# Weights at two distances from the activations, down projections each in their own product order, and inputs laid out on the host

## The chip, the cores and the metric

The kernel runs as one program on one core of one Trainium2 chip. The metric is the device time of that core in microseconds (us), the median of several executions. The engines are PE (TensorE: MATMUL, and LDWEIGHTS, which the profile lists apart as PEld), DVE (VectorE), ACT (ScalarE), POOL (GpSimd) and SP (SyncE, which issues nearly all DMAs here).

## The reference

256 tokens of width 1024 go through four blocks. Everything is float32.

```
x = x + even_mixer(rmsnorm(x))   # z = h @ w_in; spatial gating and latent attention; @ w_out
x = x + swiglu(rmsnorm(x))       # (silu(h @ w_gate) * (h @ w_up)) @ w_down, hidden width 2816
x = x + odd_mixer(rmsnorm(x))    # retention with 4 heads, output gate, @ w_out
x = x + swiglu(rmsnorm(x))
twice: a layer of  x = layer_norm(alpha*x + 0.5*ffn(x)),
                   x = layer_norm(alpha*x + mixer(x)),      # delta rule, two attentions, gates
                   x = layer_norm(alpha*x + 0.5*ffn(x))     # each ffn: swiglu, hidden width 4096
```

The work is nearly all matrix products of the 256 tokens with weights that are read once from HBM: 409 MB of them.

## The kernel before

**Products.** A float32 product is made of three products in `fp32r`, a format that PE takes at full rate. Each operand is split into a rounded `hi` and the rest, `lo`; computed are w_hi·a_hi, w_hi·a_lo and w_lo·a_hi. ACT writes `whi` from the raw weights (`upper`, L1266), DVE writes `wlo = raw - whi` (L2026), and the same is done for activations (`xx` holds xh and xl of the normed input, `H` the hidden values, `RX` a copy of x times the norm's gain with two more columns).

**Three forms of the inner loop.** In what follows, k is a slice of 128 input features.
- *Pair* (`mm2`, used by `gemm_wide`, `gemm_first(wide)` and the down projections in `ffn`): xh and xl of a k stand beside each other, so one MATMUL of 512 columns does whi with both (a *hi* product), and one of 256 columns does wlo with xh (a *lo* product). The variable `turn` flips at each pair, so PE runs hi lo, lo hi, hi lo, lo hi: two hi, two lo, and so on.
- *Triple* (`mm3`): hi, lo, hi of 256 columns each (258 with `RX`).
- *Tokens* (`gemm_tm`, `down_tokens`): the activations are the stationary operand and 512 columns (some 384 or 324) of weights the moving one; hi, hi, lo.

For every MATMUL an LDWEIGHTS brings its 128x128 stationary operand while the MATMUL ahead of it runs.

**Order and buffers.** All engines run written programs. SP loads the chunks of `ORDER` (128 partitions x 4 KB) into 6 buffers `raw`; `whi` and `wlo` have 5 slots each of 4096 bytes per partition. PE takes chunk after chunk with `weights`, waiting for DVE's `wlo`. A PSUM bank is taken with `take`, which waits for its last readers.

**Where things lie in SBUF.** `line(past)` in `lay_memory` pads so that the next tensor begins `past` bytes after a multiple of 512. The slices of whi, wlo, xx and H that a product takes begin at multiples of 512 bytes from their tensor's start, so what `line` gives is what counts. Before: whi 0, wlo 0, xx 64, H 64, all mod 512. Counted in steps of 64 bytes, weights and activations are an odd distance (1) apart, hi and lo alike. `RX` begins at 128 mod 512 and its rows are 1032 bytes long, so its slices shift by 8 or 16 bytes with each row and sweep through all distances.

**The start.** SP issues x (1 MB, tokens on partitions), the constants `cst`, the packed gains `pk`, then the first weights `ew_c`. PE waits for x and cst and turns x with 16 transposes (L1231), four to a bank; DVE copies each bank to `m.x` (`take_in`, L2039). ACT and DVE then write xh (L1288) and xl (L2086), scaled by a gain out of pk. Before its second product PE needs chunk 1: ACT's whi comes in its program behind the eight xh, DVE's wlo behind the eight xl.

**Sums over features for the norms.** `rms_stats` multiplies a matrix of 1/1024 (`onm`, plain float32) with two tiles of partial sums of squares (`t8[0]` and `t8[1]` or `t8[7]`) into one bank; at two of the four places it does the same in columns (`ps<-onc,t`). The retention head does so with `ones` and two tiles of `osq`. The weights of the spatial gating, `gw`, are turned on PE (L787).

Of the kernel before, what the change touches and what calls it, by code (L numbers as in the profile page):

```python
# [14 lines left out]
ALPHA = float(4.0 ** 0.25)  # L15
NEG = -1e30
# [224 lines left out]
def lay_memory(nc, ctx, plan):  # L241
# [38 lines left out]
    at = line(64)  # L280
# [6 lines left out]
    at = line(64)  # L287
# [4 lines left out]
    m.RX = nc.alloc_sbuf_tensor_at("RX", [128, 8, 2, 258], F32R, offset=at + 65600, align_bytes=64)  # L292
# [12 lines left out]
    m.xtm = c.get(2, 1024)  # L305
    m.sqt = arena[:, 0:2048]
# [39 lines left out]
    c = Carve(arena, nar, at=16432)  # L346
# [7 lines left out]
    names = ["x", "cst", "pk", "lvm", "out"] + [f"raw{i}" for i in range(NRAW)]  # L354
# [12 lines left out]
    "trx",  # L367
# [66 lines left out]
def tensor_program(e, m):  # L434
# [121 lines left out]
    def rms_stats(st, RT=False, last=1, bank=7):  # L556

        acc = [m.t8[0], m.t8[last]]
        w.wait_ge(s["acc"], st)
        if last == 7:  # L560
            w.wait_ge(s["xsq"], st, 7)
        b = take(bank, ("root", st))
        mm(b[:, 0:256], m.onm, acc[0], start=True, stop=False)
        mm(b[:, 0:256], m.onm, acc[1], start=False, stop=True).then_inc(s["stat"].h, s["stat"].up(st))
        if RT:
            b = take(6, ("root", st, "T"))
            for tt in range(2):
# [20 lines left out]
    def gemm_raw(st, spec, at):  # L588
# [8 lines left out]
        def tile(n, k):  # L597
# [3 lines left out]
            return mm3(b[:, 0:258], wh[:, c:c + 128], wl[:, c:c + 128], a[:, 0, :], a[:, 1, :], k == 0, k == 7)  # L601
# [22 lines left out]
    def down_tokens(st, wd):  # L624

        def tile(c, tt, wh, wl):
            b = bt[tt]
            for kk in range(2):
                k, cols, sl = c % 16 * 2 + kk, slice(kk * 512, kk * 512 + 512), slice(tt * 128, tt * 128 + 128)
                w.wait_ge(s["hlo"], st, k)  # L630
                mm(b[:, :], m.H[:, k, 0, sl], wh[:, cols], start=False, stop=False)
                mm(b[:, :], m.H[:, k, 1, sl], wh[:, cols], start=False, stop=False)
                t = mm(b[:, :], m.H[:, k, 0, sl], wl[:, cols], start=False, stop=k == 31)
# [21 lines left out]
        for c in range(12, 16):  # L655
            tile(c, 1, *wv[c - 12]).then_inc(s["gemm"].h, s["gemm"].up(wd, 16 + c))

    def ffn(st, wg, wu, wd, nt, kind, then, ln, at=0):
# [23 lines left out]
        for n in range(8):  # L682
            b = take(b0 + n % 4, ("xadd", then, n))
            for k in range(nt):
                if k % 8 == 0:
                    wh, wl = weights(wd, n * down_chunks(nt) + k // 8)
                w.wait_ge(s["hlo"], st, k)
                c = k % 8 * 128
                t = mm2(b, wh[:, c:c + 128], wl[:, c:c + 128], m.H[:, k], k == 0)
                if k % 8 == 7 or k == nt - 1:  # L690
                    t.then_inc(s["gemm"].h, s["gemm"].up(wd, n * down_chunks(nt) + k // 8))
# [49 lines left out]
    def even():  # L741
# [27 lines left out]
        value(0)  # L769
        w.wait_ge(s["edve"], "kpf")  # L770
# [104 lines left out]
    def odd():  # L875
        for cg in range(4):
            bq = [take(2 * (cg % 2) + tt, ("ract", "v", cg, tt)) for tt in range(2)]
            gemm_tm("ow_v", cg * 4, bq, xh, xl, 8, 2, 512, st="o")
            if cg == 0:
                rms_stats("o", RT=True, last=7)  # L880
# [5 lines left out]
        def head(h):  # L886
# [23 lines left out]
            mm(b[:, 0:256], m.ones, m.osq[:, 0, :], start=True, stop=False)  # L910
            mm(b[:, 0:256], m.ones, m.osq[:, 1, :], start=False, stop=True).then_inc(s["rps"].h, s["rps"].up("sum", h))
# [313 lines left out]
    w.wait_ge(s["cst"], "in")  # L1225
    w.wait_ge(s["x"], "in")
    for p in range(4):
        b = take(p, ("xadd", "in", p))
        for kk in range(2):
            for tt in range(2):  # L1230
# [2243 lines left out]
```

## Time and profile before

| | |
|---|---|
| median of 3 runs | 2294.93 us (2294.81 to 2295.20) |
| the profiled execution: its own time | 2295.12 us |
| its span in the trace | 2293.3 us |
| PE busy | 2275.4 us, 99% |
| PEld busy | 2060.9 us, 90% |
| DVE busy | 1783.0 us, 78% |
| ACT busy | 1287.0 us, 56% |
| HBM traffic | 179 GB/s over the span |

The profiled execution took 1.8 us more than its span, which lie before the first and after the last instruction. PE is busy from end to end; matmuls are pipelined, so the duration of one (about 160 ns longer than the distance to the next one's start) doesn't add up, and the rate is read from start to start.

### The profile page before, as it was taken

The page shows a single profiled execution, that of the slowest core. Times are in us where ns is not written, and L with a number is a line of the kernel's source. Part 1 is how long each engine was busy: PE and PEld are TensorE (multiplying, and loading weights), DVE is VectorE, ACT ScalarE, POOL GpSimd, SP SyncE. Part 2 cuts the span into 40 slices and gives each one's busy share as a digit, 9 for nine tenths or more (in the row PEclk, how much of TensorE's full clock was granted, in tenths as well). Part 3 has the DMA queues.
Part 4 walks back from the last instruction along what each step waited for, and adds up shares of the span by engine and source line. Part 5 has one row for each costly group of instructions (what it writes and reads, how often), then busy time and mean ns, then how long its engine had stood idle before and what let it go on. Part 6 is the DMA issues. An engine that isn't in the chain of part 4 may idle for free.

```text
span 2293.3 us, 37657 instructions
## 1 busy us (share of the span) xinstructions
PE 2275.4 (99%) x15127; PEld 2060.9 (90%) x15127; DVE 1783.0 (78%) x2709; ACT 1287.0 (56%) x2017; POOL 79.7 (3%) x96
## 2 busy tenths in 40 slices
PE   8999999999999999999999999999999999999998
PEld 7988889998888888999999888998889999998887
DVE  6989658779859876797679886698767976798854
ACT  6855455655445554585656554455545856565542
POOL 0012000002100000020000000000000200000000
PEclk9999999999999999999999999999999999999999
DMA  6456565456556556654355555556665543556563
GB/s 229 141 186 196 190 203 172 153 162 208 183 177 211 193 188 190 201 180 137 120 184 183 195 191 182 178 193 204 186 195 195 182 139 121 177 182 218 188 184 99
DMA packets 115452, 412.45 MB, mean 180 GB/s; under 512 B 12880, under 2 KB 14800, under 8 KB 115024
## 3 DMA queue, kind: packets, MB, share of 16 engines
q1 hardware_dynamic: 114992, 407.96, 54.8%
q8 instruction: 120, 1.97, 0.4%
q0 software_dynamic: 288, 2.10, 0.3%
q14 instruction: 52, 0.43, 0.1%
HBM read 408.96 MB, written 1.05 MB: 179 GB/s over the span
## 4 chain that ended last, share of the span: by engine, by line
PE 88%; DVE 8%; ACT 2%; issue 1%; DMA 0%; SPq 0%; POOL 0%; DVEq 0%; ACTq 0%
PE ps L452 87%; DVE wlo L2026 3%; DVE region L2817 1%; ACT whi L1266 1%; ACT region L1487 1%; PE ps L725 0%; DMA raw<-in_ew_c 0%; DVE region L2348 0%; DVE RX L2218 0%; DVE x L2078 0%; DVE region L2351 0%; DVE x L2225 0%; DVE region L2463 0%; DVE region L2490 0%; DVE region L2986 0%
## 5 line engine op out<-in xcount | busy, mean ns | idle before, releaser
L452 PE MATMUL ps<-xx,whi 128*128 128x512 f32 (+1 forms) x4504 | 1204.3, 353 | 2.6 <-DVE wlo L2026 1.7
L2026 DVE TENSOR_TENSOR wlo<-raw,whi 128x1024 fp32r<-128x1024 f32 (+3 forms) x772 | 925.9, 1208 | 268.8 <-ACT whi L1266 266.8
L1266 ACT ACTIVATE whi<-raw 128x1024 fp32r<-128x1024 f32 (+3 forms) x772 | 801.0, 1043 | 520.9 <-PE ps L452 507.6
L452 PEld LDWEIGHTS ps<-xx,wlo 128*128 128x128 f32 x3696 | 694.3, 188 | 118.8 <-DVE wlo L2026 0.2
L452 PE MATMUL ps<-xx,wlo 128*128 128x256 f32 x3696 | 797.2, 279 | 0.0
L452 PEld LDWEIGHTS ps<-xx,whi 128*128 128x128 f32 x4504 | 691.5, 188 | 8.3 <-issue 4.9
L452 PE MATMUL ps<-H,whi 128*128 128x512 f32 (+1 forms) x2144 | 538.6, 339 | 0.1
L452 PE MATMUL ps<-H,wlo 128*128 128x256 f32 x1632 | 363.9, 279 | 0.0
L452 PEld LDWEIGHTS ps<-H,wlo 128*128 128x128 f32 x1632 | 306.5, 188 | 46.8
L452 PEld LDWEIGHTS ps<-H,whi 128*128 128x128 f32 x2144 | 329.4, 188 | 1.6 <-issue 0.8
L2021 DVE TENSOR_REDUCE t<-ps 128x256 f32<-128x512 f32 x320 | 219.8, 688 | 40.7 <-PE ps L452 36.5
L1414 ACT ACTIVATE H<-t 128x256 fp32r<-128x256 f32 x172 | 72.0, 418 | 96.3 <-DVE t L2379 41.7
L1449 ACT ACTIVATE t<-t 128x256 f32<-128x256 f32 x160 | 65.6, 410 | 60.2 <-DVE t L2419 33.0
L452 PE MATMUL ps<-whi,H 128*128 128x512 f32 (+1 forms) x296 | 91.8, 391 | 0.0
L452 PE MATMUL ps<-region 128*128 128x128 f32 (+9 forms) x944 | 89.4, 272 | 0.0
L452 PE MATMUL ps<-RX,whi 128*128 128x258 f32 x480 | 89.3, 285 | 0.0
L2049 DVE TENSOR_TENSOR H<-t,H 128x256 fp32r<-128x256 f32 x179 | 74.4, 419 | 10.5 <-ACT H L1414 7.3
L452 PEld LDWEIGHTS ps<-region 128*128 128x128 f32 (+5 forms) x944 | 76.0, 158 | 6.6
L452 PE MATMUL ps<-whi,xx 128*128 128x512 f32 (+1 forms) x288 | 79.4, 360 | 0.0
L452 PEld LDWEIGHTS ps<-RX,whi 128*128 128x128 f32 x480 | 75.5, 191 | 0.1
L3193 POOL TENSOR_TENSOR t<-t,R 128x256 f32<-128x256 f32 x44 | 53.6, 1219 | 561.2 <-ACT t L1449 561.2
L452 PE MATMUL ps<-RX,wlo 128*128 128x258 f32 x240 | 68.0, 283 | 0.0
(311 smaller groups left out, 1561.4 us busy)
## 6 DMA issues: line engine op xcount, KB each, us to landing
raw<-in_sg SPq DMA_DIRECT2D x128, 512.0 KB, 3.5
raw<-in_su SPq DMA_DIRECT2D x128, 512.0 KB, 3.5
raw<-in_sd SPq DMA_DIRECT2D x128, 512.0 KB, 4.0
raw<-in_mw_g SPq DMA_DIRECT2D x48, 512.0 KB, 3.5
raw<-in_fg SPq DMA_DIRECT2D x44, 512.0 KB, 3.2
raw<-in_fu SPq DMA_DIRECT2D x44, 512.0 KB, 3.3
raw<-in_fd SPq DMA_DIRECT2D x32, 512.0 KB, 3.5
raw<-in_mw_a SPq DMA_DIRECT2D x24, 512.0 KB, 4.1
```

Of the source, the lines that this page charges most:

```text
L452: return e.matmul(out, lhsT, rhs, start=start, stop=stop, skip_group_check=True)
L1266: e.activation(m.whi[:, c % NHL, 0:cw], m.raw[:, c % NRAW, 0:cw], ACT.Copy).then_inc(s["whi"].h, s["whi"].up(c))
L1414: e.activation(m.H[:, j, 0, :], m.t2[:, j % 4, :], ACT.Copy, scale=-0.5 if raw(j) else 1.0).then_inc(s["hhi"].h, s["hhi"].up(st, j))
L1449: e.activation(g, g, ACT.Silu).then_inc(s["silu"].h, s["silu"].up(st, j))
L1487: e.activation(S[:, i, sl], S[:, i, sl], ACT.Exp, bias=st[:, 1, c:c + 1], accum_out=st[:, 2, c:c + 1]).then_inc(s["aact"].h, s["aact"].up( ...
L2021: return e.tensor_reduce(dst, b[:, :].rearrange("p (a b) -> p b a", a=2), AX, ALU.add)
L2026: e.tensor_tensor(m.wlo[:, c % NHL, 0:cw], m.raw[:, c % NRAW, 0:cw], m.whi[:, c % NHL, 0:cw].bitcast(F32), ALU.subtract).then_inc(s["wlo"] ...
L2049: e.tensor_tensor(dst, src, hi.bitcast(F32), ALU.subtract).then_inc(s[sig[1]].h, s[sig[1]].up(*key))
L2817: e.scalar_tensor_tensor(y[:, d:256], pr[:, 0:256 - d], pk(f"cw{l}", 12 * (3 - d) + i), y[:, d:256], ALU.mult, ALU.add).then_inc(s["cdve"] ...
L3193: e.tensor_tensor(g, g, m.R[:, 0, :], ALU.mult).then_inc(s["fnrm"].h, s["fnrm"].up(st, j))
```

## The change

- `lay_memory`: whi now begins at 64, wlo at 128, x at 128, xx, t12 and H at 192, mod 512. In steps of 64 bytes the distance to xx and H is 2 for whi and 1 for wlo. `RX` gets rows of 288 (1152 bytes), of which 258 are used, and begins at 320 mod 512: 4 steps from whi, 3 from wlo, and every further slice an even number of steps on. `Hs` is H moved on by 64 bytes, used by the last feed-forward (`t1`) alone, whose down projection is of the tokens form: 3 steps from whi, 2 from wlo.
- `row` takes the place of `mm2` in the down projections: within a chunk it runs `RUN[st]` hi products and as many lo ones, and flips at each group (at run 1 it is always hi, lo). RUN is 2, 1, 4, 8, 2 for f0, f1, s00, t0, s01.
- x comes turned from the host, in two halves that ACT's DMA queue loads straight into `m.x`; the 16 transposes and `take_in` are gone, and in their place PE runs 14 products of `onm` with itself (WARM) which nobody reads. pk and cst move behind the first and the third weight chunk in SP's queue; `gmw` comes turned from the host.
- In the four `rms_stats` and the four retention heads DVE adds the two tiles into one, so that PE sums one.

```
+WARM = 14
+RUN = {"f0": 2, "f1": 1, "s00": 4, "t0": 8, "s01": 2}
     m.raw = sb("raw", [128, NRAW, CW])
-    line(0)
+    line(64)
     m.whi = sb("whi", [128, NHL, CW], F32R)
-    line(0)
+    line(128)
     m.wlo = sb("wlo", [128, NHL, CW], F32R)
-    line(0)
+    line(128)
     m.x = sb("x", [128, 8, 256])
-    line(64)
+    line(192)
     m.xx = sb("xx", [128, 8, 2, 256], F32R)
...
-    m.RX = nc.alloc_sbuf_tensor_at("RX", [128, 8, 2, 258], F32R, offset=at + 65600, align_bytes=64)
+    m.RX = nc.alloc_sbuf_tensor_at("RX", [128, 8, 2, 288], F32R, offset=at + 65664, align_bytes=64)
+    m.Hs = nc.alloc_sbuf_tensor_at("Hs", [128, 32, 2, 256], F32R, offset=at + 64, align_bytes=64)
...
+    def row(st, b, wh, wl, c, ks, run):
+
+        for i in range(0, len(ks), run):
+            turn[0] ^= 1
+            for lo in (0, 1) if turn[0] or run == 1 else (1, 0):
+                for k in ks[i:i + run]:
+                    w.wait_ge(s["hlo"], st, 8 * c + k)
+                    o, wt = (b[:, 0:256], wl) if lo else (b[:, :], wh)
...
-        mm(b[:, 0:256], m.onm, acc[0], start=True, stop=False)
-        mm(b[:, 0:256], m.onm, acc[1], start=False, stop=True).then_inc(s["stat"].h, s["stat"].up(st))
+        mm(b[:, 0:256], m.onm, acc).then_inc(s["stat"].h, s["stat"].up(st))
...
+    def two_to_one(st):
+
+        w.wait_ge(s["acc"], st, 2)
+        e.tensor_tensor(m.t8[0], m.t8[0], m.t8[1], ALU.add).then_inc(s["acc"].h, s["acc"].up(st))
...
-    w.wait_ge(s["cst"], "in")
-    w.wait_ge(s["x"], "in")
-    for p in range(4):
...
+    for _ in range(WARM):
+        mm(ps[7][:, 0:128], m.onm, m.onm)
...
+    for p in range(2):
+        e.dma_start(m.x[:, 4 * p:4 * p + 4, :], ins["x"][:, 4 * p:4 * p + 4, :]).then_inc(
+            s[f"x{p}"].h, s[f"x{p}"].up("in", by=16))
```

The start on DVE, before (L2039 is `take_in`, L2086 writes xl, L2026 wlo, L2122 to L2128 add the squares):

```order
L3154 CAST onc<-one 128x1
L2039 COPY x<-ps 128x512 x2
L2026 TENSOR_TENSOR wlo<-raw,whi 128x1024
L2086 SCALAR_TENSOR_TENSOR xx<-x,pk,xx 128x256 x2
L2039 COPY x<-ps 128x512
L2086 SCALAR_TENSOR_TENSOR xx<-x,pk,xx 128x256 x2
L2039 COPY x<-ps 128x512
L2086 SCALAR_TENSOR_TENSOR xx<-x,pk,xx 128x256 x4
L2026 TENSOR_TENSOR wlo<-raw,whi 128x1024 x3
L2122 TENSOR_TENSOR t<-t 128x512
```

and after:

```order
L3151 CAST onc<-one 128x1
L2022 TENSOR_TENSOR wlo<-raw,whi 128x1024
L2077 SCALAR_TENSOR_TENSOR xx<-x,pk,xx 128x256 x8
L2022 TENSOR_TENSOR wlo<-raw,whi 128x1024 x3
L2114 TENSOR_TENSOR t<-t 128x512
L2117 TENSOR_TENSOR t<-t 128x512
L2120 TENSOR_TENSOR t<-t 128x512
L2083 TENSOR_TENSOR t<-t 128x256
```

The four copies are gone; the sum of squares has one more step (L2083).

SP's queue at the start, before:

```order
L3251 DMA region<-in_x 128x2x1024
L3251 DMA cst<-in_consts 128x768
L3251 DMA pk<-in_pack 128x359
L3290 DMA raw<-in_ew_c 128x1024 x4
L3251 DMA rowc<-in_rowa 128x704
```

and after (the two halves of x are at the head of ACT's program, beside these):

```order
L3286 DMA raw<-in_ew_c 128x1024
L3246 DMA pk<-in_pack 128x359
L3286 DMA raw<-in_ew_c 128x1024 x2
L3246 DMA cst<-in_consts 128x768
L3286 DMA raw<-in_ew_c 128x1024
```

The first weight chunk no longer stands behind 1.6 MB of other loads in its queue.

PE at the turn from the last gate and up products to the down projection of f0, before:

```order
L452 MATMUL ps<-xx,wlo 128x256 x2
L452 MATMUL ps<-xx,whi 128x512
L452 MATMUL ps<-H,whi 128x512
L452 MATMUL ps<-H,wlo 128x256 x2
L452 MATMUL ps<-H,whi 128x512 x2
```

and after:

```order
L453 MATMUL ps<-xx,wlo 128x256 x2
L453 MATMUL ps<-xx,whi 128x512
L453 MATMUL ps<-H,whi 128x512 x2
L453 MATMUL ps<-H,wlo 128x256 x4
L453 MATMUL ps<-H,whi 128x512 x4
```

Groups of two became groups of four; in f1 they are of one, in t0 of sixteen. The number and the shapes of these products stay the same.

## Rows read from the trace of the kernel before

**Rows 1.** The page: span, and busy time of each engine (share, instructions).

```profile
span 2293.3 us, 37657 instructions
...
PE 2275.4 (99%) x15127; PEld 2060.9 (90%) x15127; DVE 1783.0 (78%) x2709; ACT 1287.0 (56%) x2017; POOL 79.7 (3%) x96
```

**Rows 2.** Waits of PE, whole span: us in total, times, longest.

```profile
PE ps L1231 <- DMA cst<-in_consts: 6.9, 1, 6.9
PE ps L452 <- DVE wlo L2026: 1.7, 5, 0.5
```

**Rows 3.** Timeline of PE in f0's down projection: start, us, tile, count.

```profile
240.12 0.62 PE L452 MATMUL ps<-H,whi 128*128 128x512 f32 x2
240.58 0.40 PE L452 MATMUL ps<-H,wlo 128*128 128x256 f32 x2
...
242.88 0.62 PE L452 MATMUL ps<-H,whi 128*128 128x512 f32 x2
```

**Rows 4.** Stretches: length, busy us of PE, PEld, DVE, ACT, POOL, clock, DMA, GB/s.

```profile
5.00:10.00 5.00, 3.07 (x15) 3.10 (x16) 1.72 (x3) 1.43 (x3) 0.00 (x0) 1.00 1.03 415
...
962.00:978.00 16.00, 16.00 (x137) 16.00 (x138) 15.40 (x34) 13.41 (x25) 0.00 (x0) 1.00 0.93 349
```

**Rows 5.** Timeline of PE in a run of triples, first and last.

```profile
387.19 0.40 PE L452 MATMUL ps<-xx,whi 128*128 128x256 f32 x2
387.43 0.28 PE L452 MATMUL ps<-xx,wlo 128*128 128x256 f32 x1
...
392.14 0.40 PE L452 MATMUL ps<-xx,whi 128*128 128x256 f32 x2
```

**Rows 6.** By tile, 240 to 290 us (pairs): duration ns min/median/max.

```profile
L452 PE MATMUL ps<-H,whi x146: 388/392/394, 239.7 to 289.8; 128*128 128x512 f32 x146
L452 PE MATMUL ps<-H,wlo x146: 276/276/283, 239.9 to 289.7; 128*128 128x256 f32 x146
```

**Rows 7.** The same view, 963 to 978 us (triples).

```profile
L452 PE MATMUL ps<-xx,whi x86: 279/280/280, 962.9 to 977.8; 128*128 128x256 f32 x86
```

**Rows 8.** The same view, whole span, tile RX.

```profile
L452 PE MATMUL ps<-RX,wlo x240: 279/283/292, 940.8 to 2032.3; 128*128 128x258 f32 x120
```

**Rows 9.** The same view, 2198 to 2230 us (tokens).

```profile
L452 PE MATMUL ps<-wlo,H x46: 393/396/398, 2198.0 to 2229.5; 128*128 128x512 f32 x46
```

**Rows 10.** Groups by form around 1023.4 us, then 39.0 us: a last MATMUL before a pause.

```profile
L452 PE MATMUL ps<-xx,whi 128*128 128x256 f32 x1 | 0.3, 276 | 0.0
...
L452 PE MATMUL ps<-wlo,xx 128*128 128x512 f32 x1 | 0.4, 390 | 0.0
```

**Rows 11.** Groups by form, whole span: count, busy us, mean ns.

```profile
L452 PE MATMUL ps<-xx,whi 128*128 128x512 f32 x2880 | 899.2, 392 | 0.0
...
L452 PE MATMUL ps<-H,whi 128*128 128x512 f32 x1120 | 348.7, 392 | 0.0
...
L452 PE MATMUL ps<-xx,whi 128*128 128x256 f32 x1616 | 303.1, 284 | 2.6 <-DVE wlo L2026 1.7 <-DVE xx L2086 0.8
...
L452 PE MATMUL ps<-H,whi 128*128 128x256 f32 x1024 | 189.9, 282 | 0.1
```

**Rows 12.** The chain that ended last, 0 to 40 us: start, us, what.

```profile
2.19 6.36 DMA raw<-in_ew_c
8.55 0.02 issue
8.57 1.07 ACT whi L1266
9.64 0.02 issue
9.66 0.43 DVE wlo L2026
...
15.59 1.24 DVE wlo L2026
16.83 0.14 issue
16.96 18.91 PE ps L452 x136
```

**Rows 13.** Timeline at the start and at two sums of squares.

```profile
10.81 0.88 DVE L2086 SCALAR_TENSOR_TENSOR xx<-x,pk,xx 128x256 fp32r<-128x256 f32 x2
...
21.64 0.69 DVE L2128 TENSOR_TENSOR t<-t 128x512 f32<-128x512 f32 x1
...
22.70 1.02 PE L452 MATMUL ps<-t,onc 128*128 128x256 f32 x4
23.56 0.95 PE L452 MATMUL ps<-onc,t 128*128 128x1 f32 x8
24.37 0.37 PE L452 MATMUL ps<-xx,whi 128*128 128x256 f32 x1
```

**Rows 14.** Groups by form, 11.3 to 15.3 and 16.9 to 22 us; timeline of transposes.

```profile
L452 PE MATMUL ps<-xx,wlo 128*128 128x256 f32 x6 | 2.5, 416 | 0.0
...
L452 PE MATMUL ps<-xx,wlo 128*128 128x256 f32 x14 | 3.9, 279 | 0.0
...
6.93 3.65 PE L1231 MATMUL ps<-cst,region 128*128 128x128 f32 x16 [6.93 <-DMA cst<-in_consts]
...
39.38 0.66 PE L787 MATMUL ps<-cst,region 128*128 128x128 f32 x4
```

More of the change, by code:

```diff
@@ L352, in sig @@
         return Sig(ctx.enter_context(nc.semaphore(f"s_{name}")), plan and plan[name])
-    names = ["x", "cst", "pk", "lvm", "out"] + [f"raw{i}" for i in range(NRAW)]
+    names = ["x0", "x1", "cst", "pk", "lvm", "out"] + [f"raw{i}" for i in range(NRAW)]
     names += ["rowa", "gmw", "cs", "mk", "cc", "ss", "dtr", "rowc", "relb", "negd", "blk", "rowe"]
@@ L656, in down_tokens @@
             tile(c, 1, *wv[c - 12]).then_inc(s["gemm"].h, s["gemm"].up(wd, 16 + c))
+    def row(st, b, wh, wl, c, ks, run):
[5 more added lines that the diff above has]
+                    o, wt = (b[:, 0:256], wl) if lo else (b[:, :], wh)
+                    a = m.H[:, 8 * c + k, 0, :] if lo else m.H[:, 8 * c + k].rearrange("p a b -> p (a b)")
+                    t = mm(o, wt[:, k * 128:k * 128 + 128], a, start=c == 0 and k == 0 and lo == (0 if turn[0] or run == 1 else 1),
+                           stop=False)
+        return t
     def ffn(st, wg, wu, wd, nt, kind, then, ln, at=0):
@@ L683, in ffn @@
             b = take(b0 + n % 4, ("xadd", then, n))
[L684 to L691, printed above, removed]
+            for c in range(down_chunks(nt)):
+                wh, wl = weights(wd, n * down_chunks(nt) + c)
+                t = row(st, b, wh, wl, c, range(min(8, nt - 8 * c)), RUN[st])
+                t.then_inc(s["gemm"].h, s["gemm"].up(wd, n * down_chunks(nt) + c))
             if ln and n == 2:
@@ L769, in even @@
         value(0)
+        w.wait_ge(s["cst"], "in")
         w.wait_ge(s["edve"], "kpf")
@@ L879, in odd @@
             if cg == 0:
-                rms_stats("o", RT=True, last=7)
+                rms_stats("o", RT=True)
         for i in range(8):
@@ L909, in head @@
             b = take(5, ("ract", "root", h))
-            mm(b[:, 0:256], m.ones, m.osq[:, 0, :], start=True, stop=False)
-            mm(b[:, 0:256], m.ones, m.osq[:, 1, :], start=False, stop=True).then_inc(s["rps"].h, s["rps"].up("sum", h))
+            mm(b[:, 0:256], m.ones, m.osq[:, 0, :]).then_inc(s["rps"].h, s["rps"].up("sum", h))
             for _ in range(4):
@@ L1407, in ffn @@
     def ffn(st, wg, wu, wd, nt, kind, tile, bname=None, first=0):
+        H = m.Hs if st == "t1" else m.H
         def raw(j):
@@ L1413, in hidden @@
             w.wait_ge(s["fmul"], st, j)
-            e.activation(m.H[:, j, 0, :], m.t2[:, j % 4, :], ACT.Copy, scale=-0.5 if raw(j) else 1.0).then_inc(
+            e.activation(H[:, j, 0, :], m.t2[:, j % 4, :], ACT.Copy, scale=-0.5 if raw(j) else 1.0).then_inc(
                 s["hhi"].h, s["hhi"].up(st, j))
@@ L1524, in even @@
             s["root"].h, s["root"].up("rr", 1))
-        w.wait_ge(s["eps"], "gw")
-        e.activation(m.gwT, four(3), ACT.Copy).then_inc(s["eact"].h, s["eact"].up("gwT"))
         def ukv(half):
@@ L2094, in sum_up @@
                 w.wait_ge(s["acc"], st, p - 2)
-            t = e.tensor_tensor(m.sqs[0], m.sqs[0], m.sqs[p], ALU.add)
-            t.then_inc(s["acc"].h, s["acc"].up(st, p - 1) if p < 3 else s["acc"].up(st))
+            e.tensor_tensor(m.sqs[0], m.sqs[0], m.sqs[p], ALU.add).then_inc(s["acc"].h, s["acc"].up(st, p - 1))
         for p in range(5):
@@ L2355, in ffn @@
         rms = kind == "rms"
+        H = m.Hs if st == "t1" else m.H
         def hidden(j):
@@ L3154, in vector_program @@
     e.tensor_copy(m.onc, m.one).then_inc(s["set"].h, s["set"].up("onm"))
-    for p in range(2):
-        take_in(p)
     lower(done[1])
```

96 lines of the change are left out of this document (39 added, 57 removed).

## The prediction

> **What bounds the kernel now.** I read the page first: PE is busy for 2275 of 2293 us [rows 1], so no other engine sets the pace. Then PE's waits: 6.9 us for the first load, 1.7 us in five waits for wlo, and little else [rows 2]. Beyond the start there is nothing to win from waits; what is left is how long PE's stream itself takes. So I looked at it from start to start. In the pair form four hi/lo laps, that is 8 pairs, go from 240.12 to 242.88: 2.76 us, 345 ns per pair [rows 3]. In the triple form 14 triples go from 387.19 to 392.14: 354 ns each, 118 per product [rows 5]. The granted clock is 1.00 there [rows 4], the level of 2.4 GHz, at which 768 columns are 320 ns: both forms lose time inside the stream, with no wait beside it.
>
> Where is it lost? By tile, the durations in one stretch of pairs aren't equal: 388 to 394 ns for hi, 276 to 283 for lo [rows 6], though shapes and sources are the same. Two MATMULs that run with no weight load beside them (the next one comes only after a pause) took 276 and 390 ns [rows 10], the low end of that spread. Triples always take 279 or 280 [rows 7], products of RX 279 to 292, median 283 [rows 8], tokens 393 to 398 [rows 9]. So I read 276 and 388 as undisturbed and the rest as what the LDWEIGHTS beside it costs. This is the part that distances in SBUF could touch.
>
> **What the distances can give, and take.** The form counts are in [rows 11]. 2880 + 1120 = 4000 pairs. The 256-column hi products, 1616 + 1024 = 2640, are two to a triple: 1320 triples, 3960 products. RX has 720 products, tokens some 650 of 512 columns.
> - Pairs: a duration exceeds the distance to the next start by 162 ns (280 against 118 in the triples). An undisturbed pair is then (388 - 162) + (276 - 162) = 340 ns, now it is 345: 4000 x 5 = 20 us to win.
> - Triples: 3.5 ns a product, 3960 x 3.5 = 14 us.
> - RX: 283 - 277 (two more columns) is 6 ns, 720 x 6 = 4 us.
> - Tokens: 395 - 390 is 5 ns, 650 x 5 = 3 us.
> The ceiling is 41 us. On the other side stand the slowest of the same rows: a pair of (394 - 162) + (283 - 162) = 353 ns, 4000 x 8 = 32 us; triples at 283, 14 us; together 46 us to lose.
>
> No row shows a product at an even distance only. The nearest is RX, which passes through even and odd ones and through places between; its median is 283 against 280 for triples at distance 1, for 2 columns (0.8 ns) more. This says that the distance is no free gift, and that some distances are worse than 1; but RX's slices are also not on a 64-byte step, which is a cause of its own. What speaks for a gain: in the pairs the same addresses give 276 in one lap and 283 in the next, so the loss hangs on how the two reads meet in time, and the two kinds of weights no longer lie alike. I take a third of the ceiling, **14 us**, as a choice between 41 won and 46 lost, with more weight on the near end of the gain.
>
> The Trainium skill ("SBUF — State Buffer", Who interferes with whom) gives PE two read ports, one for the moving operand and one for LDWEIGHTS, independent, and says that PE never waits on anyone. By that rule the distances give 0. The trace doesn't quite agree: 276 ns without a load beside it, 279 to 283 with one.
>
> **The order in the down projections.** The products stay the same in number and shape. Between pairs as now (345) and like next to like (triples' 118 and tokens' 233, from 395 less the 162 ns by which a duration exceeds the distance to the next start: 351), 6 ns a pair. Long groups are in s00 and t0, 512 pairs: at most 3 us lost. As much could be won. I take 0.
>
> **The start.** Now: ew_c lands at 8.55, 6.36 us after its issue, since x, cst and pk, 1.6 MB, are ahead of it; ACT's whi and DVE's wlo follow, then xl, and the second chunk lets PE go at 16.96, from where on it doesn't stop [rows 12]. The load path is full: 415 GB/s from 5 to 10 us [rows 4]. 2.15 MB were in at 8.55, so at this rate the bytes count from 3.4 us. After: the first ew_c and half of x, 1.05 MB, share the path: 5.9 us. pk with as much of x's second half, 0.37 MB more: 6.8 us. ACT's whi 5.9 to 7.0; wlo on DVE to 8.2; then eight xl at 0.44 [rows 13], no longer held up by copies and transposes, to 11.7; wlo of the second chunk 1.2 more, and PE goes on at 12.9 instead of 16.96: **4.1 us** won; 2.5 if pk comes late through the shared path, 5 if it comes first. Until 15.3 the products last 416 ns against 279 later [rows 14]: the low level of the clock, at which a distance is 0.21 us instead of 0.12. WARM puts PE to work from 1.2 us: each of its 14 float32 products is two instructions, and the transposes show 3.65 / 16 = 0.23 us for one of 128 columns at the low level [rows 14], so the 28 end at 7.6 us at the latest, before wlo is there at 8.2; they cost nothing. If the clock is low at 8.7 us, the first 24 products need 0.64 us per k in place of 0.44, and PE ends some 0.5 us later.
>
> **Work taken from PE.** A float32 product of 256 columns is two instructions, 0.215 us each: four of them from 22.70 to 23.56 [rows 13]. Half goes in four norms and four heads: 8 x 0.43 = 3.4 us. The eight `onc,t` take 0.81 us (23.56 to 24.37), half goes, at two places: 0.8. Four transposes of gw: at most 0.66 - 0.16 = 0.5 [rows 14]. Sum **4.7 us**, all on the stream, so all won. What it adds is one DVE add of about 0.45 us in each chain. At the first norm this bites: DVE ended the sum at 22.33, PE came for it at 22.70. After, PE comes 4.1 us earlier, ACT's squares only some 3.9, and the add and its wait are 0.5: PE waits 0.3. At the other norms and in the heads the sum is there microseconds before PE asks, by the order in which the programs stand. Behind DVE's added step are queued the wlo of later chunks, five slots ahead.
>
> **The sum.** 2295.12 - 14 (distances) - 0 (order) - 4.1 (start) - 4.7 (PE work) + 0.3 = 2272.6. The profiled run is 0.2 above the median: **2272.4 us**.
>
> **Rivals.**
> - *The distances do nothing.* The loss stays, or only changes places between products, so that the durations of [rows 6 to 9] keep their means. Then the sum is 2286.6 in the profiled run, 2286.4 as a median. For it: RX's rows, which show no distance that is free; against it: the spread from 276 to 283 at one pair of addresses. The rule of the Trainium skill named above would give this too. Still faster, by 0.4%. Chance 0.22, with 2281 to 2290.
> - *The even distance costs.* Hi loads then meet the moving reads at each step rather than in every other lap: hi at 394, triples' products at 283. It decides from 0.7 ns a product: 9 us won elsewhere over 12,700 products; it is slower by 0.2% from 1.0 ns (13 us). At 2 ns on average the time is 2286 + 25 = 2311. For it: RX, the only tile off distance 1, is the slowest; against it: RX is off the 64-byte steps too, and lo keeps its odd distance. Chance 0.13, of which 0.09 beyond +0.2%.
> - *The distances free the stream entirely:* 41 us, 2245. Chance 0.10 for anything below 2251.
> - *The start is not faster,* because ACT's queue and SP's share the path and pk comes last: it would take up to 3 us off, and changes nothing else. It is in the ranges.
> My forecast, 2251 to 2281, has 0.55.
>
> **The range.** 2246 to 2292 leaves out the far end of the gain (0.05) and most of the loss (0.12). About 0.2% is what a measurement of this kernel can tell from no change, 4.6 us. Faster by more: forecast, the full gain and the rival of 0, and a little of the loss: 0.85. Within: 0.06. Slower: 0.09.
>
> **What would show it.** In the profile after: xx,whi of 256 columns in triples below 279 (right) or at 280 and more; median of hi in pairs below 392; RX at 280 or less. PE's run without pauses from about 12.9 us. Two `t<-t,onc` instructions where there were four, and a wait of 0.3 us before the first. If the products' durations are unchanged and the time is 2286, the distances were no cause; if f1's or t0's pairs differ by more than 3 ns from f0's, I was wrong to take the order as nothing.

## The result: slower, and the profile after

| | before | after |
|---|---|---|
| median, four runs each on one chip | 2295.05 us | 2313.99 us (2313.33 to 2314.75) |
| ratio to before, 95% interval | | 1.0082 [1.0069, 1.0096] |
| span of the profiled execution | 2293.3 us | 2312.3 us |

The change costs 18.9 us. 2272.4 was forecast, with a range to 2292: the time lies outside it, on the other side of "before". Of the rivals, *the even distance costs* gave 2311 at 2 ns a product. One later execution, of the kernel with the new places alone, took 2584.4 us at a granted clock of 0.815 and is left out; all others compared here had 0.998 to 1.000.

The page of after, which answers to [rows 1]:

```profile
span 2312.3 us, 37627 instructions
PE 2299.5 (99%) x15111; PEld 2074.2 (90%) x15111; DVE 1786.3 (77%) x2713; ACT 1287.1 (56%) x2016; POOL 79.9 (3%) x96
```

PE has 16 instructions fewer and is busy for 24 us more. The waits of PE answer to [rows 2]:

```profile
PE ps L453 <- DVE xx L2077: 2.1, 1, 2.1
PE ps L453 <- DVE onc L3151: 1.2, 1, 1.2
PE ps L453 <- DVE wlo L2022: 1.1, 4, 0.3
...
PE ps L453 <- DVE t L2083: 0.2, 1, 0.2
```

No wait explains the loss: these are 4.6 us in seven waits, where the first load and wlo alone took 8.6 in [rows 2], and the two rows left out have 0.9 each, where before has 1.1 and 0.8. The loss is in the stream. The timeline of PE in the wide products, in the form of [rows 3] (start, length, instructions of one kind in a row):

```profile
519.84 0.41 PE L453 MATMUL ps<-xx,wlo 128*128 128x256 f32 x2
520.08 0.62 PE L453 MATMUL ps<-xx,whi 128*128 128x512 f32 x2
520.54 0.40 PE L453 MATMUL ps<-xx,wlo 128*128 128x256 f32 x2
...
522.66 0.41 PE L453 MATMUL ps<-xx,wlo 128*128 128x256 f32 x2
```

It goes on like this, two and two; from 519.84 to 522.66 are 8 pairs in 2.82 us, 352.5 ns each, where [rows 3] gave 345. The tiles of the same kernel tell which products; columns are count, duration in ns as min/median/max, first and last start. First the pairs on xx from 520 to 600 us, before and after:

```profile
L452 PE MATMUL ps<-xx,whi x233: 388/392/394, 519.7 to 599.7; 128*128 128x512 f32 x117
L452 PE MATMUL ps<-xx,wlo x233: 276/276/283, 519.9 to 599.9; 128*128 128x256 f32 x117
```

```profile
L453 PE MATMUL ps<-xx,whi x229: 388/397/402, 519.6 to 600.0; 128*128 128x512 f32 x115
L453 PE MATMUL ps<-xx,wlo x228: 278/282/286, 519.8 to 599.6; 128*128 128x256 f32 x114
```

Hi goes from 392 to 397, and lo, whose distance is still 1, from 276 to 282. In the same 80 us stand 229 hi products in place of 233. Then two down projections of after, f0 (RUN 2) and f1 (RUN 1), the same view as [rows 6]:

```profile
L453 PE MATMUL ps<-H,whi x165: 392/397/398, 230.8 to 288.7; 128*128 128x512 f32 x165
L453 PE MATMUL ps<-H,wlo x165: 280/284/287, 231.0 to 288.9; 128*128 128x256 f32 x165
```

```profile
L453 PE MATMUL ps<-H,wlo x166: 278/280/283, 616.8 to 674.0; 128*128 128x256 f32 x166
L453 PE MATMUL ps<-H,whi x165: 391/392/393, 616.9 to 673.7; 128*128 128x512 f32 x165
```

From start to start over the whole stage these are 353.3 ns a pair in f0 and 346.7 in f1. Triples, in two stretches of after, beside [rows 7]:

```profile
L453 PE MATMUL ps<-xx,whi x29: 276/278/282, 53.0 to 57.9; 128*128 128x256 f32 x29
L453 PE MATMUL ps<-xx,wlo x14: 276/279/284, 53.1 to 57.6; 128*128 128x256 f32 x14
```

```profile
L453 PE MATMUL ps<-xx,whi x58: 282/283/285, 969.8 to 980.0; 128*128 128x256 f32 x58
L453 PE MATMUL ps<-xx,wlo x28: 281/281/282, 970.0 to 979.7; 128*128 128x256 f32 x28
```

Places and form are the same in both, yet a product takes 116.7 ns from start to start in the first and 120 in the second; each stretch keeps to one of the two.

The trace of before has two rates as well, at its own places and at a granted clock of 1.00. [rows 7] and the prediction's "triples always take 279 or 280" hold for most of its triples, not for all. These are its triples on H from 473 to 481 us, and those of the same stage from 482 us on:

```profile
L452 PE MATMUL ps<-H,whi x47: 279/280/467, 472.6 to 480.9; 128*128 128x256 f32 x47
L452 PE MATMUL ps<-H,wlo x23: 278/279/279, 472.9 to 480.7; 128*128 128x256 f32 x23
```

```profile
L452 PE MATMUL ps<-H,whi x57: 276/276/276, 481.9 to 491.4; 128*128 128x256 f32 x57
L452 PE MATMUL ps<-H,wlo x29: 276/276/276, 481.8 to 491.3; 128*128 128x256 f32 x29
```

The first run at 117.8 ns a product, the second at 113.3, the rate that the prediction calls undisturbed. Between them lie two products that started 0.4 and 0.2 us after the one ahead; no address and no order changed.

I summed the distances between starts by form over the whole trace:

| form | before, us | after, us | difference |
|---|---|---|---|
| pairs on xx (5776 products found) | 998.3 | 1019.0 | +20.7 |
| pairs on H (2240) | 386.5 | 392.6 | +6.1 |
| triples, xx and H (3960) | 480.8 | 481.3 | +0.5 |
| tokens of 512 columns | 151.6 | 150.2 | -1.3 |
| RX | 89.9 | 90.0 | +0.1 |
| the rest of the span (start, sums, transposes, other forms) | | | -7.1 |

The last row is what is left of the 19.0 us between the two spans. So the loss is in the pairs, 27 us, and the start and the work taken from PE give back 7.

The start did nearly what was forecast. The timeline of after, PE and what it waits for, beside [rows 12] and [rows 13]:

```profile
1.18 5.58 PE L453 MATMUL ps<-onc 128*128 128x128 f32 x28 [1.18 <-DVE onc L3151]
...
6.10 1.06 ACT L1260 ACTIVATE whi<-raw 128x1024 fp32r<-128x1024 f32 x1 [2.96 <-DMA raw<-in_ew_c]
...
8.33 3.25 DVE L2077 SCALAR_TENSOR_TENSOR xx<-x,pk,xx 128x256 fp32r<-128x256 f32 x8
...
8.86 0.39 PE L453 MATMUL ps<-xx,whi 128*128 128x256 f32 x1 [2.09 <-DVE xx L2077]
...
18.99 0.28 PE L453 MATMUL ps<-xx,whi 128*128 128x256 f32 x1
19.44 0.70 PE L453 MATMUL ps<-t,onc 128*128 128x256 f32 x2 [0.17 <-DVE t L2083]
19.97 0.50 PE L453 MATMUL ps<-onc,t 128*128 128x1 f32 x4
20.34 0.36 PE L453 MATMUL ps<-xx,whi 128*128 128x256 f32 x1
```

### The profile page after: what moved, and what is told of

It reads as the page before. It is cut to its first block, busy times and chain, and to the rows that moved or that the text cites. A ratio compares the mean times of both kernels' runs of the same rounds, so it can differ in the third digit from the quotient of the medians.

```text
span 2312.3 us, 37627 instructions
## 1 busy us (share of the span) xinstructions
PE 2299.5 (99%) x15111; PEld 2074.2 (90%) x15111; DVE 1786.3 (77%) x2713; ACT 1287.1 (56%) x2016; POOL 79.9 (3%) x96
## 4 chain that ended last, share of the span: by engine, by line
PE 87%; DVE 9%; ACT 3%; issue 1%; DMA 0%; SPq 0%; POOL 0%; DVEq 0%; ACTq 0%
PE ps L453 86%; DVE wlo L2022 3%; DVE region L2814 1%; ACT whi L1260 1%; ACT region L1482 1%; DMA raw<-in_ew_c 0%; PE ps L731 0%; DVE region L2341 0%; DVE RX L2211 0%; DVE x L2069 0%; DVE region L2344 0%; DVE x L2218 0%; DVE region L2457 0%; DVE region L2484 0%; DVE region L2983 0%
## 5 line engine op out<-in xcount | busy, mean ns | idle before, releaser
L453 PE MATMUL ps<-xx,whi 128*128 128x512 f32 (+1 forms) x4504 | 1217.1, 356 | 3.3 <-DVE xx L2077 2.1
L453 PE MATMUL ps<-xx,wlo 128*128 128x256 f32 x3696 | 808.0, 282 | 0.0
L453 PEld LDWEIGHTS ps<-xx,whi 128*128 128x128 f32 x4504 | 698.7, 188 | 8.5 <-issue 3.3
L453 PE MATMUL ps<-H,whi 128*128 128x512 f32 (+1 forms) x2144 | 498.7, 342 | 0.0
L453 PEld LDWEIGHTS ps<-H,whi 128*128 128x128 f32 x2144 | 359.5, 188 | 36.6 <-issue 0.7
L453 PE MATMUL ps<-H,wlo 128*128 128x256 f32 x1632 | 329.9, 281 | 0.0
L453 PEld LDWEIGHTS ps<-H,wlo 128*128 128x128 f32 x1632 | 263.0, 188 | 14.7
L1409 ACT ACTIVATE H<-t 128x256 fp32r<-128x256 f32 x140 | 58.5, 418 | 73.8 <-DVE t L2373 28.3
L453 PE MATMUL ps<-whi,Hs 128*128 128x512 f32 x256 | 80.8, 398 | 0.0
L2040 DVE TENSOR_TENSOR H<-t,H 128x256 fp32r<-128x256 f32 x150 | 62.2, 419 | 9.4 <-ACT H L1409 5.8
```

The lines of the kernel that those rows point to most:

```text
L453: return e.matmul(out, lhsT, rhs, start=start, stop=stop, skip_group_check=True)
L1409: e.activation(H[:, j, 0, :], m.t2[:, j % 4, :], ACT.Copy, scale=-0.5 if raw(j) else 1.0).then_inc(s["hhi"].h, s["hhi"].up(st, j))
L2040: e.tensor_tensor(dst, src, hi.bitcast(F32), ALU.subtract).then_inc(s[sig[1]].h, s[sig[1]].up(*key))
```

## The experiments

Places are written as (distance of whi, distance of wlo) from the activations, in steps of 64 bytes: before is (1,1), the change (2,1). Each label stands for one kernel; those without an interval ran once, beside runs of before with medians of 2295.0 to 2295.3. So differences of 1 to 3 us between such kernels rest on the sums and distances of their traces more than on the one time.

**The new places alone.** All the `line` offsets, `RX` and `Hs` of the change, and nothing else of it.

```
-    line(0)
+    line(64)
     m.whi = sb("whi", [128, NHL, CW], F32R)
-    line(0)
+    line(128)
     m.wlo = sb("wlo", [128, NHL, CW], F32R)
-    line(0)
+    line(128)
     m.x = sb("x", [128, 8, 256])
-    line(64)
+    line(192)
     m.xx = sb("xx", [128, 8, 2, 256], F32R)
```

> The kernel before with the new places in SBUF alone (whi 64, wlo 128, x 128, xx, t12 and H 192 mod 512, RX in rows of 288, Hs for the last down projection); start, sums and product orders as before. Theory A, the places cost and nothing else does: pairs over xx at 353 ns as in the changed kernel, pairs over H, which keep the old alternation, at 353 too (the changed kernel has 347 to 353 there), and a time of 2313.99 plus the 9 us of start and sums that are missing here: 2318 to 2326 us. Theory B, the loss comes from the product orders or from the state in which the new start leaves PE: pairs stay at 345 ns and the time is within 5 us of 2295.

Measured: 2323.08 us, 1.0121 [1.0104, 1.0138]. 27.9 us are lost by the addresses alone; pairs take 352.5 ns, on xx and on H alike. The tile of xx has the medians of the changed kernel, 397 and 282.

**All but the places.** The changed kernel with the offsets of before (whi, wlo, x at 0, xx and H at 64, `RX` with rows of 258, `Hs` on H).

> The changed kernel with the places of before (whi 0, wlo 0, xx and H 64 mod 512, RX in rows of 258, no Hs); new start, new sums, new product orders. Theory A (the places cost): pairs over xx back at 345 ns, and the time is 2295.0 less the 9 us of start and sums, plus or minus 3 us for the orders: 2283 to 2289 us, faster than both. Theory B (orders or start cost): pairs over xx stay near 353 ns and the time stays above 2305.

Measured: 2288.20 us, 0.9970 [0.9959, 0.9981]: 7 us faster than before. The tile has the durations of before again:

```profile
L453 PE MATMUL ps<-xx,whi x233: 388/392/395, 519.8 to 599.8; 128*128 128x512 f32 x117
L453 PE MATMUL ps<-xx,wlo x232: 275/278/283, 520.0 to 599.5; 128*128 128x256 f32 x116
```

**The orders alone.** Before, with `row` and RUN (2, 1, 4, 8, 2) in the down projections.

```
+                t = row(st, b, wh, wl, c, range(min(8, nt - 8 * c)), RUN[st])
-                t = mm2(b, wh[:, c:c + 128], wl[:, c:c + 128], m.H[:, k], k == 0)
```

> The kernel before with only the down projections' product orders changed (groups of 2, 1, 4, 8, 2). If like beside like is the slow case, as the triples and tokens suggested, the pairs over H go from 345 ns to about 347 (groups of 2 and 4) and 351 (groups of 8), and the time is 2296 to 2299 us. If an order can also be the better one at the old places, group 1 shows it: f1's pairs below 345 ns. If orders do nothing: 345 everywhere, 2295 us.

Measured: 2296.89 us, 1.7 slower than before. From start to start a pair takes 345.9 ns in f0 (run 2), 353.2 in f1 (run 1), 344.6 in s00 (4), 344.8 in t0 (8); before has 345.0 everywhere. Run 1 is the only order that costs more than 1 ns, and it is the order that did well at the new places (346.7). Its tile in f1, where after had 392 and 280:

```profile
L453 PE MATMUL ps<-H,whi x166: 392/397/399, 616.7 to 675.0; 128*128 128x512 f32 x166
L453 PE MATMUL ps<-H,wlo x165: 278/282/286, 616.9 to 674.9; 128*128 128x256 f32 x165
```

Now the account can be closed, by form, since one thing stands in the way of plain differences: with the same order and places, f1's pairs took 353.2 ns here and 348.9 in the kernel with all but the places. The stage can run at two rates, as the triples did, so the 8.7 us between those two kernels hold some 2 us of such states.
- Places: 2323.08 - 2295.15 = +27.9 us, of which pairs on xx +20.8, pairs on H +8.3, tokens -1.4.
- Orders, in the pairs on H: +1.6 us at the old places (388.1 against 386.5), -2.2 at the new (392.6 against 394.7).
- Start and work taken from PE, as what is left beside the forms: 2313.99 - 2323.08 = -9.1, less the -2.2 of the orders and the +0.3 by which the triples differ between these two kernels, is **-7.2 us**.

**Is it parity?** If each even distance costs, then two of them cost more than one, and moving which of the two is even changes little. Four kernels, all of them before with other offsets:

```
         whi  wlo  x    xx, t12, H      distances
before     0    0    0   64             (1,1)
             0   64   64  192             (3,2)
             0    0    0  128             (2,2)
             0    0    0  192             (3,3)
             0  128  128  192             (3,1)
```

> The kernel before with whi 0, wlo 64, x 64, xx, t12 and H 192 mod 512: whi is 3 steps of 64 bytes from xx and H, wlo 2 steps. All else as before. Theory A1, it is the hi weights at an even distance that cost: here hi is odd and pairs are at 345 ns or below, 2290 to 2296 us. Theory A2, it is the mix of an even and an odd distance that costs, or any even one: pairs at 349 to 354 ns, 2312 to 2330 us. Theory A3, only the exact distance of 1 is good, parity says nothing: pairs at neither value.

Measured: 2314.74 us; pairs 350.0 ns, triples 354.6.

> The kernel before with whi and wlo 0, xx, t12 and H 128 mod 512: whi and wlo are both 2 steps of 64 bytes from xx and H. So far pairs took 345.0 ns at (whi 1, wlo 1), 352.5 at (2, 1), 350.0 at (3, 2). Theory P, the parity of each load's distance decides and even ones collide: both even is the worst, pairs at 357 ns or more (7.5 + 5.0 above 345), about 2340 us. Theory M, it is that whi and wlo lie differently to each other which costs: both even is as good as both odd, 345 ns, 2295 us.

Measured: 2310.31 us; pairs 348.3 ns, triples 356.4 on average.

> The kernel before with whi and wlo 0, xx, t12 and H 192 mod 512: both are 3 steps from xx and H. Theories P (parity) and M (whi and wlo alike) both expect 345.0 ns per pair and 2295 us, to 1 us. Theory D, the exact distance matters and not its parity: pairs at another value, off by 2 ns or more.

Measured: 2296.33 us; pairs 346.7 ns; triples 353.3 in most stretches, but 340 to 343 in many, 348.3 on average.

> The kernel before with whi 0, wlo 128, xx, t12 and H 192 mod 512: whi 3 steps from xx and H, wlo 1, both odd, yet 2 steps apart from each other. Theory P: 345.0 ns per pair, 2295 us. Theory M in its strict form (any difference between whi and wlo costs): 350 to 353 ns, 2314 to 2325 us. Theory D: another value.

Measured: 2291.87 us; pairs 346.7 ns, triples 342.2 on average and 340.0 over long stretches. The tiles of (3,2), (2,2) and (3,1) in the same 80 us, one after the other:

```profile
L452 PE MATMUL ps<-xx,whi x230: 392/392/398, 519.8 to 599.8; 128*128 128x512 f32 x115
L452 PE MATMUL ps<-xx,wlo x228: 277/280/285, 520.3 to 599.5; 128*128 128x256 f32 x114
```

```profile
L452 PE MATMUL ps<-xx,wlo x231: 278/279/281, 519.8 to 599.9; 128*128 128x256 f32 x116
L452 PE MATMUL ps<-xx,whi x230: 387/392/398, 519.9 to 599.6; 128*128 128x512 f32 x115
```

```profile
L452 PE MATMUL ps<-xx,whi x232: 388/390/392, 519.7 to 599.9; 128*128 128x512 f32 x116
L452 PE MATMUL ps<-xx,wlo x232: 281/282/283, 519.9 to 599.7; 128*128 128x256 f32 x116
```

No simple rule holds. A cost for each even distance would put (2,2) above (2,1)'s 352.5, near 357, and a cost for unlike distances would put it at 345; it is 348.3. Two odd distances aren't free either: (3,3) and (3,1) have 346.7, not 345. But an even one is in each of the three slow cases, and (3,1) stands out: most of its triples run at 113.3 ns a product, the rate of products without any disturbance. Triples at (1,1) and (3,3) have it in some stretches only, those at (2,1) and (2,2) nowhere.

**Does the place itself matter, or only the distance?** Before with everything moved on by 64 bytes: whi, wlo, x at 64, xx and H at 128.

> The kernel before with whi, wlo and x at 64 and xx, t12 and H at 128 mod 512: everything 64 bytes further on, the distances (1, 1) as before. If only the distance between weights and activations matters, pairs stay at 345.0 ns, triples at 353.3 and the time at 2295 us, to 1 us. If the places themselves matter (an even or odd line for one of the two reads), pairs and triples change by 1 ns or more.

Measured: 2294.32 us, pairs 345.0 ns, as before. For the pairs only the distance matters. The triples are 1.0 us shorter in sum: from 401.8 to 408.9 us they take 276 ns where before, with the same products, has 280. Of the two rates that before shows at 473 and 482 us, a stretch can take one in one kernel and the other in the next.

**A better order at the old places.** The second kernel of this section with RUN 4 in all five down projections.

> The changed kernel with the places of before and groups of 4 in all five down projections. With groups of 1 f1's pairs took 353.2 ns at the old places, with 2 345.9, with 4 344.6, with 8 344.8. From the 2288.2 us of the same kernel with the mixed groups: f1's 176 pairs win 8.6 ns each (1.5 us), f0's and s01's 1.3 ns (0.6 us). Expected 2286.0 us, 2285.3 to 2286.8. If the group's price hangs on the stage or on the history and not on its size, f1 does not come to 344.6 ns.

Measured: 2287.28 us (2287.07 to 2287.45), 0.9966 [0.9954, 0.9979]. That misses the expected range by some 0.5 us: s00, t0 and s01 have 344.6, but f0 and f1, whose chunks hold 8, 8 and 6 slices, stay at 345.8. Most of the miss is in the start of the sum: it took f1 from 353.2 ns, which is what run 1 had with the orders alone, but in the kernel that RUN 4 was put into, f1 was at 348.9. So f1 won 0.5 us where 1.5 were expected. The gain over the mixed orders is 0.9 us. Here the pairs are where before has them (1384.6 us in all against 1384.8) and the triples 0.7 lower, so of the 7.9 us won 7.0 are start and work taken from PE, beside the 7.2 above.

**A map.** A kernel that leaves out all work of this one but products on PE: 152 sections of 32 slices each, 64 times pairs in the alternation of before and 64 times triples, over 8 by 8 distances, and 24 with hi and lo in groups.

```
    wlo = {d: wl[:, 16 * d:16 * d + 1024] for d in range(8)}
    a = {d: ac[:, 16 * d:16 * d + 4096].rearrange("p (k a b) -> p k a b", a=2, b=256) for d in range(8)}
    for n, (form, dh, dl) in enumerate(SECTIONS):
        act, lo = a[dh], wlo[(dh - dl) % 8]
```

> No model at all, only PE: 152 sections of 32 slices of matmuls on one set of weights and activations, each at its own pair of distances (whi, wlo to the activations, in steps of 64 bytes), the moving and the stationary operand never written in between. Sections 1 to 64: pairs in the old alternation (hi lo, lo hi) for all distances 0 to 7 of whi and of wlo; 65 to 128: triples for the same; then pairs in groups of 1, 2, 4 and 8 at six pairs of distances. It leaves out all other work, so its output is not the reference's. If distances alone set the rate, it repeats the kernel's: pairs 345.0 at (1, 1), 352.5 at (2, 1), 348.3 at (2, 2), 350.0 at (3, 2), 346.7 at (3, 1) and (3, 3); triples 353.3 at (1, 1), 340 to 343 at (3, 1). If other engines' use of SBUF has a part in it, all sections are near 340, the undisturbed rate, and alike.

Measured, ns per slice of 128 features from start to start, over whole laps. A lap is the number of products after which the distances between starts repeat: 3 to 16 in this table, so a count that ends inside one can be off by 2 to 3 ns. Pairs, then triples; the table repeats after 4 steps, 256 bytes, in both directions, to 0.1 ns in the triples and 0.8 in the pairs (the very first section is left out):

| whi \ wlo | 0 | 1 | 2 | 3 | | 0 | 1 | 2 | 3 |
|---|---|---|---|---|---|---|---|---|---|
| 0 | 348.3 | 346.7 | 350.0 | 350.0 | | 360.0 | 353.3 | 357.3 | 353.3 |
| 1 | 349.6 | 345.0 | 350.0 | 351.7 | | 353.3 | 353.3 | 346.7 | 356.7 |
| 2 | 353.3 | 352.5 | 348.6 | 353.3 | | 355.0 | 360.0 | 356.0 | 360.0 |
| 3 | 356.5 | 346.7 | 350.0 | 346.7 | | 353.3 | 340.0 | 354.7 | 353.3 |

The pairs have the kernels' rates to 0.3 ns: 345.0 at (1,1), 352.5 at (2,1), 348.6 at (2,2), 350.0 at (3,2), 346.7 at (3,1) and (3,3). The place of before, (1,1), has the lowest pairs of all 16; that of the change, (2,1), is fourth from the slow end in the pairs and level with the slowest triples. Groups of one, two and four give the following: (1,1) has 353.3, 345.8 and 344.6, (2,1) has 346.7, 353.3 and 348.9. So run 1 is bad at the first and good at the second, run 2 the other way round, with the numbers that f0 and f1 had in the kernels. For run 8 the map says nothing: its sections are too short to show a lap repeat, and over the 32 products of one lap the figure goes from 342.0 to 348.0 at (1,1) and from 345.4 to 351.2 at (2,1) with where the count begins. In the kernels t0 had 344.8 and 350.4.

The map has one rate for each place, since every section begins in the same way. It doesn't show the second rate that the kernels have: 340.0 for triples at (1,1) from 482 us on, and 350 in place of 360 at (2,1).

The rows of the map, first pairs at (1,1) and at (2,1), then triples at (2,1) and at (3,1):

```profile
L58 PE MATMUL ps<-act,wlo x24: 276/278/283, 115.8 to 123.5; 128*128 128x256 f32 x24
L58 PE MATMUL ps<-act,whi x24: 388/392/394, 116.0 to 123.8; 128*128 128x512 f32 x24
```

```profile
L58 PE MATMUL ps<-act,wlo x24: 278/282/285, 207.0 to 214.9; 128*128 128x256 f32 x24
L58 PE MATMUL ps<-act,whi x23: 388/397/401, 206.8 to 214.6; 128*128 128x512 f32 x23
```

```profile
L58 PE MATMUL ps<-act,whi x46: 282/283/284, 941.9 to 950.0; 128*128 128x256 f32 x46
L58 PE MATMUL ps<-act,wlo x23: 281/281/281, 941.8 to 949.7; 128*128 128x256 f32 x23
```

```profile
L58 PE MATMUL ps<-act,whi x49: 276/276/276, 1034.8 to 1043.0; 128*128 128x256 f32 x49
L58 PE MATMUL ps<-act,wlo x24: 276/276/276, 1035.1 to 1042.9; 128*128 128x256 f32 x24
```

Nothing but PE runs in that kernel, so no other engine and no DMA is needed for the effect: what changes from section to section is only the distance of a product's moving operand from the weights that are loaded beside it. That the two reads meet is what this points to; no row shows the meeting.

**What the map points to.** At (3,1) three products of 256 columns take 340.0 ns, less than one of 512 and one of 256 anywhere in the left half. So: the changed kernel at (3,1), and every pair written as a triple.

```
-        turn[0] ^= 1
-        if turn[0]:
-            mm(b[:, :], wh, a.rearrange("p a b -> p (a b)"), start=start, stop=False)
-            return mm(b[:, 0:256], wl, a[:, 0, :], start=False, stop=True)
-        mm(b[:, 0:256], wl, a[:, 0, :], start=start, stop=False)
-        return mm(b[:, :], wh, a.rearrange("p a b -> p (a b)"), start=False, stop=True)
+        mm(b[:, 0:256], wh, a[:, 0, :], start=start, stop=False)
+        mm(b[:, 0:256], wl, a[:, 0, :], start=False, stop=False)
+        return mm(b[:, 256:512], wh, a[:, 1, :], start=False, stop=False)
```

> The changed kernel with whi 0, wlo 128, xx, t12 and H 192 mod 512, distances (3, 1), RX and H as before, and every pair written as three products of 256 columns: whi with xh, wlo with xh, whi with xl into the bank's second half, which leaves all readers as they are. In the map a triple at (3, 1) takes 340.0 ns, the undisturbed rate, and a pair at its best place 343 to 345. If the map holds in the kernel: the 4060 slices of pairs go from 346.7 ns at (3, 1) to 340 to 341, 23 to 27 us; from 2291.87 less 8.7 for start and sums that is 2256 to 2261 us. If more LDWEIGHTS (half as many again in the pairs) cost something that the map did not show, for instance against the other engines' accesses, the former pairs stay above 343 ns and the time above 2268.

Measured: 2258.17 us (2258.11 to 2258.96), 0.9839 [0.9824, 0.9854]: 37 us faster than before and 56 than the change, with 4000 more products. Page and tile:

```profile
span 2256.2 us, 45627 instructions
PE 2239.7 (99%) x19111; PEld 2191.0 (97%) x19111; DVE 1781.3 (79%) x2713; ACT 1285.7 (57%) x2016; POOL 79.2 (4%) x96
```

```profile
L453 PE MATMUL ps<-xx,whi x465: 275/276/277, 519.9 to 598.8; 128*128 128x256 f32 x155
L453 PE MATMUL ps<-xx,wlo x233: 275/277/277, 519.8 to 598.7; 128*128 128x256 f32 x117
```

Against (3,1) with pairs, all products on xx and H took 1861.6 us there and 1834.7 here, 26.9 less; the start and the work taken from PE give the 7 known. Together 33.9, against 2291.87 - 2258.17 = 33.7 measured. Weight loads are now busy 97% of the span; whether a further split of products would run into them wasn't tried.

**RX at (3,1) too.** The same with `RX` in rows of 320, which puts all its slices on the same two distances.

```
-    m.RX = nc.alloc_sbuf_tensor_at("RX", [128, 8, 2, 258], F32R, offset=at + 65600, align_bytes=64)
+    m.RX = nc.alloc_sbuf_tensor_at("RX", [128, 8, 2, 320], F32R, offset=at + 65536, align_bytes=64)
```

> The same with RX in rows of 320 (1280 bytes) that begin at 192 mod 512, so that all its slices are 3 steps from whi and 1 from wlo too, in place of sweeping through the distances. Its 720 products of 258 columns are then undisturbed at 114 to 115 ns rather than 121 to 123: 5 us less than the run beside it. If RX's loss had to do with its length of 258 columns and not with its place, no change.

Measured: 2258.03 us, 0.9838 [0.9821, 0.9854], no gain where 5 us were expected. RX with rows of 258, then with rows of 320:

```profile
L453 PE MATMUL ps<-RX,wlo x240: 276/283/289, 920.1 to 1998.7; 128*128 128x258 f32 x120
```

```profile
L453 PE MATMUL ps<-RX,wlo x240: 278/282/288, 920.0 to 1998.5; 128*128 128x258 f32 x120
```

120.7 ns a product against 120.3. The places are those at which 256 columns run at 113.5, and in all kernels above, whatever their offsets, RX has 119.9 to 120.7. So RX's loss doesn't hang on its address. That leaves its 258 columns, but no run gives RX's stage 256, so this is argued and not shown.

## Why the prediction was wrong

**What bounds the kernel: right.** The stream of PE set the time in every kernel here, and the reading that durations above 276 and 388 are loss beside weight loads held: products at 276/276/276 run at 113.3 ns. In the kernel built on them, all products on xx and H take 30.9 us less than before (1865.6 to 1834.7), where 34 were the ceiling for pairs and triples; 7 more come from the start and the work taken from PE. "Triples always take 279 or 280" was misread: at (1,1) they also ran at 276 for 10 us, so part of the triples' loss was there to win without moving anything.

**The distances: the step that failed.** The term was -14, within -41 and +46, and measured +27.9. The bounds were sound; the choice between them was not. Two readings led to it. "The same addresses give 276 in one lap and 283 in the next, so the loss hangs on how the two reads meet in time" is in line with the runs, and speaks for neither sign: by it another distance gives another meeting, not a better one. I took the near end of the gain from it. And the one row off distance 1, RX with 283, was set aside as off the 64-byte steps; the last run shows that it said nothing of distances at all, as it stays at 282 to 283 on them. So no row of before bore on an even distance, and the honest term was near zero with both signs open. It would still have named the wrong side.

**The rival that came in** was *the even distance costs*, 2311 forecast, 2314.0 measured, at a chance of 0.13. Its price of 2 ns a product was about right: 27.9 us over 12,700 products are 2.2. That price was a choice, and its nearness is luck in part, since its picture was not right. "Lo keeps its odd distance" was to spare the lo products, but their median rose from 276 to 282, the hi ones' from 392 to 397. And the triples, for which it had 283 against 280, lost 0.5 us in all: about half of their stretches went from 353 ns to 350 and below, the others to 355 and 360. Parity isn't the rule either, as the map shows: it is the two distances together, modulo 256 bytes, with the form and the order of the products.

The Trainium skill ("SBUF — State Buffer", Who interferes with whom) has PE's two read ports independent and PE waiting on no one, by which the distances give 0. The runs disagree: with the same instructions in the same order, (3,1) takes 2291.9 us and (2,1) 2323.1.

**The orders: zero was near in sum, wrong in its parts.** +1.6 us at the old places, -2.2 at the new, within the 3 either way. The test that the prediction set, f1 or t0 over 3 ns from f0, came out: f1 is 346.7 against 353.3. The reason given, like next to like at 351 against 345, was taken from other forms; groups of four and eight measured 344.6 and 344.8 at the old places. What counts is the pair of order and distances: run 1 costs 8 ns at (1,1) and gains 6 at (2,1).

**The start and the work taken from PE: right in kind, somewhat short.** Forecast -4.1 - 4.7 + 0.3 = -8.5, measured -7.0 to -7.2, about 1.4 short. PE was through with the products before the first norm's sum at 19.11 us (18.99 + 0.12), where it began the sum at 22.70 before: 3.6 us in place of 4.1. The 0.5 short is what the prediction had named as possible: WARM's 28 instructions ended at 6.76, PE stood idle from then to 8.86, and from 9.4 to 12.6 the products ran at 0.21 us from start to start, the low level of the clock (granted: 0.50 from 9.5 to 12.3). WARM had raised the clock, as its last instructions, from 5.8 us on, stood 0.11 us apart in place of 0.21, and one product behind the pause still took 0.12; then it fell. PE then waited from 19.11 to 19.44, the 0.3 forecast, though the profile puts only 0.17 of it to the wait. Two `t<-t,onc` stand where four did, four `onc,t` where eight did, and the product behind them starts at 20.34 in place of 24.37: 4.0 us. Some 3.9 were forecast from the other sums and gw, and 3.1 came; which of them gave less wasn't taken apart.

**The sum.** 2295.1 + 27.9 (places) - 2.2 (orders) - 7.2 (start and work) + 0.3 (triples) = 2313.9, against 2314.0 measured. With the forecast's other terms as they were, the first alone decided the sign.

## What to carry to other kernels

When PE's stream is full, compare durations of one form with that of a product that runs alone: the difference is what the weight loads beside it cost, and it can be moved by addresses. But its sign can't be argued: map the distances of both weights from the moving operand over 256 bytes, with the form and the order of the products that the kernel uses, in one kernel that does nothing else, before a layout is chosen. Count over whole laps, and check the choice in the kernel, where a stretch can run at a second rate. And let the form be free in that map: here three products of 256 columns at (3,1) beat one of 512 and one of 256 at every distance.

## What the runs showed of the hardware

- The time of fp32r products beside weight loads depends on the distance between the two operands in SBUF modulo 256 bytes: 340.0 to 360.0 ns for three of 256 columns, 345.0 to 356.5 for one of 512 and one of 256. Moving everything together leaves the pairs as they are (345.0 and 345.0).
- The same places and order can run at two rates: triples at (2,1) at 116.7 ns a product in one stretch of the changed kernel and at 120 in another, triples at (1,1) at 117.8 and then 113.3 within one stage of before, where two products started late between them. What chooses the rate was not tested.
- 512 + 256 columns ran undisturbed at no place of the map, 345.0 ns being the least; 256 three times did at (3,1) alone in the map, and in some stretches of the kernels at (1,1) and (3,3) too. Products of 258 columns took 120.3 ns at (3,1), those of 256 took 113.5.
- What happens inside when the two reads meet isn't shown by any run; the map and the two rates are all there is.
